# The memory tile of a transformer block: loaded in 32-token strips and turned by VectorE's block transposes, where TensorE turned it

## The reference, cut to what matters

```python
mem_n = rms_norm(mem, norm_mem_src[l])        # mem: 256 x 2048
kv = (mem_n @ w_kv).reshape(b, m, 2, MEM_HEADS, MEM_HEAD_DIM)   # w_kv: 2048 x 1024
k, v = kv[:, :, 0], kv[:, :, 1]
```

## Time and profile before

| | |
|---|---|
| median of the runs | 1356.27 us |
| the profiled execution's own time | 1355.84 us |
| its span, from the first instruction to the last | 1354.1 us |
| TensorE busy | 998.5 us (74%) |
| VectorE busy | 579.0 us (43%) |
| ScalarE busy | 300.4 us (22%) |
| GpSimd busy | 52.4 us (4%) |
| the queue of the hardware DMAs, share of 16 engines | 88.7% |
| read from HBM | 481.14 MB |
| mean granted TensorE clock | 0.873 |

### The profile page before, as it was taken

One profiled execution on the slowest core, in us unless ns is written; L12 is line 12 of the kernel. 1 busy time (PEld: TensorE's weight loads), 2 busy tenths in 40 slices (PEclk: granted clock), 3 DMA queues, 4 the chain that ended last, 5 costly groups with the idle time before them and its releaser, 6 DMA issues.

```text
span 1354.1 us, 20680 instructions
## 1 busy us (share of the span) xinstructions
PE 998.5 (74%) x8540; PEld 600.2 (44%) x8540; DVE 579.0 (43%) x1114; ACT 300.4 (22%) x521; POOL 52.4 (4%) x108
## 2 busy tenths in 40 slices
PE   8999999999999985666655566655566654566656
PEld 7888898888888532222212222222222221222222
DVE  5555566886657543223332233332223332223324
ACT  5554457674455100000000000000000000000002
POOL 1300001231000000000000000000000000000001
PEclk9999999999999998778787787787777877777878
DMA  7778763448869999999999999999999999999997
GB/s 247 263 238 255 217 167 123 144 136 273 286 252 338 358 417 428 433 430 432 433 430 434 432 432 434 433 429 433 429 434 432 433 433 433 430 432 430 433 426 303
DMA packets 78020, 486.40 MB, mean 359 GB/s; under 512 B 9943, under 2 KB 25437, under 8 KB 64798
## 3 DMA queue, kind: packets, MB, share of 16 engines
q1 hardware_dynamic: 77484, 483.46, 88.7%
q10 hardware_dynamic: 306, 2.11, 0.4%
q0 software_dynamic: 192, 0.31, 0.2%
HBM read 481.14 MB, written 4.72 MB: 359 GB/s over the span
## 4 chain that ended last, share of the span: by engine, by line
PE 51%; DMA 46%; SPq 1%; DVE 1%; issue 1%; ACT 0%; DVEq 0%; ACTq 0%
DMA gu<-in_w_up 42%; PE ps L1052 10%; PE ps L605 8%; PE ps L607 8%; PE ps L606 8%; PE ps L1107 5%; DMA down<-in_w_down 4%; PE ps L1031 2%; PE ps L1064 1%; PE ps L585 1%; PE ps L850 1%; PE ps L851 1%; PE ps L852 1%; PE ps L778 1%; SPq L470 0%
## 5 line engine op out<-in xcount | busy, mean ns | idle before, releaser
L1052 PE MATMUL ps<-gu,xe 128*32 128x256 f32 x3968 | 286.3, 452 | 306.0 <-DMA gu<-in_w_up 305.5
L2138 DVE TENSOR_TENSOR x_sum<-ps,x_sum 128x512 f32<-128x512 f32 x240 | 149.1, 684 | 507.6 <-PE ps L1064 507.6
L1052 PEld LDWEIGHTS ps<-gu,xe 128*32 128x32 f32 x3968 | 140.5, 129 | 469.3 <-DMA gu<-in_w_up 328.7
L1616 DVE TENSOR_TENSOR w_lo<-w_raw,w_hi 128x1024 fp32r<-128x1024 f32 (+1 forms) x137 | 164.6, 1208 | 118.1 <-ACT w_hi L1225 114.8
L605 PE MATMUL ps<-w_hi,a_hi 128*128 128x512 f32 (+1 forms) x468 | 183.4, 392 | 0.0
L606 PE MATMUL ps<-w_lo,a_hi 128*128 128x512 f32 (+1 forms) x468 | 179.7, 384 | 0.0
L607 PE MATMUL ps<-w_hi,a_lo 128*128 128x512 f32 (+1 forms) x460 | 176.8, 384 | 0.0
L1225 ACT ACTIVATE w_hi<-w_raw 128x1024 fp32r<-128x1024 f32 (+1 forms) x137 | 141.8, 1039 | 127.1 <-PE ps L607 88.6
L1535 ACT ACTIVATE sg<-ps 128x128 f32<-128x128 f32 x31 | 8.6, 278 | 654.3 <-PE ps L1052 654.3
L1107 PE MATMUL ps<-down,act_t 128*32 128x512 f32 x976 | 112.8, 603 | 5.3 <-DMA down<-in_w_down 5.3
L606 PEld LDWEIGHTS ps<-w_lo,a_hi 128*128 128x128 f32 x468 | 88.0, 188 | 16.4
(11 more groups left out here) (341 smaller groups left out, 854.9 us busy)
## 6 DMA issues: line engine op xcount, KB each, us to landing
down<-in_w_down SPq DMA_DIRECT2D x29, 4096.0 KB, 22.7
gu<-in_w_gate SPq DMA_DIRECT2D x28, 4096.0 KB, 31.7
gu<-in_w_up SPq DMA_DIRECT2D x28, 4096.0 KB, 41.0
w_raw<-in_w_in SPq DMA_DIRECT2D x56, 512.0 KB, 4.9
w_raw<-in_w_out SPq DMA_DIRECT2D x32, 512.0 KB, 4.7
gu<-in_w_up SPq DMA_DIRECT2D x18, 512.0 KB, 6.6
w_raw<-in_w_mem_kv SPq DMA_DIRECT2D x16, 512.0 KB, 3.5
down<-in_w_down SPq DMA_DIRECT2D x13, 512.0 KB, 15.5
```

What stands on the lines that cost most here:

```text
L1052: mm = pe.matmul(ps[5][j * SLOTS:(j + 1) * SLOTS, 0:2 * P].rearrange("s (m f) -> s m f", m=2), xe[:, k, :], gu[side][:, :, k, j * P:(j + 1 ...
L1616: ve.tensor_tensor(w_lo[:, u % RING, :, 0:n], w_raw[:, u % RING, :, 0:n], w_hi[:, u % RING, :, 0:n], ALU.subtract).then_inc(S("w_split"), 1)
L2138: ins = ve.tensor_tensor(x_sum[:, t, cols], ps[g][:, :], (x_res if first else x_sum)[:, t, cols], ALU.add)
```

## The change

Memory is loaded in eight DMAs of 32 tokens each, issued by SP behind the weight loads of units 22 to 29. A token's 2048 features are cut into four quarters q of 512, and quarter q of token s goes to partition 32q + s. A block transpose of VectorE, in place, on 128 x 512 turns each 32 x 32 block, after which partition 32q + r holds feature 512q + 32k + r of every token, in block k. So block column k is a contraction tile of 128 features (four runs of 32, from the four quarters), and the rows of w_mem_kv and the gain norm_mem_src are loaded in that order. PE's 32 transposes, their PSUM banks and the waits on them go. ACT squares eight strips of 512 elements (four after SB_K, four after SB_K+1), which leaves a sum for each quarter on each partition; POOL spreads these over a 128 x 256 tile, and two matmuls with a column of ones add them up for each token. DVE's transposes come four after SB_V and four after SB_V+1. The norm's factor moves ahead of attention on POOL's queue.

The core of the diff. Left out are the hunks that only count semaphores up by one (`sums_made`, `squares_summed`) for the new sum.

```diff
@@ -87,6 +87,7 @@
 EARLY_AT = [START[W_OUT + 2] + 4 + 2 * n for n in range(12)] + [START[MEM_Q] + 5 + n for n in range(4)]
+MEM_AT = [START[SB_Q] + 6 + _j for _j in range(SEQ // QUAD)]
 LATENT = [(c, i) for c in range(Q_PE, MEM_K) for i in range(chunk_tiles(c) // UK)]
@@ -111,7 +112,7 @@
         _b = len(SPLIT_BANK)
-        SPLIT_BANK.append(6 + _b % 2 if _name == "mem" else 4 + _b % 4)
+        SPLIT_BANK.append(None if _name == "mem" else 4 + _b % 4)
@@ -205,8 +206,11 @@
         c_kv = place("c_kv", [P, TT, KV_RANK + ROPE])
-        mem_junk = place("mem_junk", [P, D], offset=km_at)
-        mem_sb = place("mem_sb", [P, TT, D], offset=o_at)
+        mem_junk = place("mem_junk", [P, UN], offset=km_at)
+        mem_spread = place("mem_spread", [P, TT * NJ, QUAD], offset=km_at + 2048)
+        quad_eye = place("quad_eye", [P, QUAD], offset=km_at + 3072)
+        mem_quads = place("mem_quads", [P, TT * NJ, UN], offset=o_at)
+        mem_turned = mem_quads[:, :, :].rearrange("p j (k s) -> p k j s", k=KD)
         cq_hi = place("cq_hi", [P, 4, SEQ], F32R, offset=k_at)
@@ -289,7 +293,8 @@
             if MEM_K <= c <= MEM_V:
-                return [cols(w_mem_kv, (c - MEM_K) * UN)]
+                return [w_mem_kv[0, :, (c - MEM_K) * UN:(c - MEM_K + 1) * UN].rearrange(
+                    "(q k r) n -> k q r n", q=NJ, r=QUAD)[i * UK:(i + 1) * UK]]
             if c < Q_PE:
@@ -370,8 +375,11 @@
                                        (norm_sb_out, 62, 8), (norm_ffn, 70, 16)):
-                    sp.dma_start(g_nat[r0:r0 + rows, :], gain[0].rearrange("(k p) -> k p", p=P)
-                                 ).then_inc(S("gains_loaded"), 16)
+                    if gain is norm_mem_src:
+                        src = gain[0].rearrange("(q k r) -> k q r", q=NJ, r=QUAD)
+                    else:
+                        src = gain[0].rearrange("(k p) -> k p", p=P)
+                    sp.dma_start(g_nat[r0:r0 + rows, :], src).then_inc(S("gains_loaded"), 16)
                 for t in range(TT):
@@ -449,7 +457,10 @@
                 (src,) = unit_src(c, i)
-                if len(src.shape) == 4:
+                if MEM_K <= c <= MEM_V:
+                    for k in range(UK):
+                        sp.dma_start(dst[:, k, :], src[k]).then_inc(S(f"w_loaded{u % RING}"), 16)
+                elif len(src.shape) == 4:
                     for k in range(UK):
@@ -457,6 +468,10 @@
                     x_part(u)
+                if u in MEM_AT:
+                    j = MEM_AT.index(u)
+                    sp.dma_start(mem_quads[:, j, :], mem[0, j * QUAD:(j + 1) * QUAD, :].rearrange(
+                        "s (q f) -> q s f", q=NJ)).then_inc(S("mem_loaded"), 16)
                 if u in MOVE_AT:
@@ -709,15 +724,17 @@
             turn(KV_LAT)
-            pe.wait_ge(S("mem_loaded"), 16)
+            pe.wait_ge(S("mem_spread"), 1)
+            for t in range(TT):
+                mm = pe.matmul(ps[7][:, t:t + 1], mem_spread[:, NJ * t:NJ * (t + 1), :].rearrange(
+                    "p j s -> p (j s)"), ones[:, 0:1], start=True, stop=True)
+            mm.then_inc(S("squares_summed"), 1)
             for n, (c, i) in enumerate(LATENT):
...
                     project_units(c, [i], 0, hi, lo)
-                if n < KD // 2:
-                    split_turn("mem", mem_sb, 2 * n, 2 * n + 2)
                 if (c, i) == (K_NOPE + 1, 0):
@@ -1325,6 +1342,15 @@
             sc.wait_ge(S("rstd"), 1)
+            def mem_squares(t):
+                for j in range(NJ):
+                    sc.wait_ge(S("mem_loaded"), 16 * TT * NJ)
+                    square(mem_quads[:, NJ * t + j, :], chunk_ss[:, t, j:j + 1], mem_junk[:, :])
+                    sq[0] += 1
+                    sc.wait_ge(S("squared"), sq[0])
             for c in range(Q_LAT, Q_PE):
@@ -1336,9 +1362,6 @@
                     squares_of(c_kv[:, :, 0:KV_RANK], SS_KV, junk[:, 0:KV_RANK])
-                    sc.dma_start(mem_sb[:, :, :], mem[0].rearrange("(t p) d -> p t d", p=P)).then_inc(
-                        S("mem_loaded"), 16)
                 elif c < SB_V:
@@ -1350,20 +1373,25 @@
                     chunk_copy(c, lambda t: v_sb[:, t, n0:n0 + UN], SS_X)
+                if SB_K <= c < SB_V:
+                    mem_squares(c - SB_K)
                 if c == SB_K:
...
                     split_head("kv", 52, hi=ckv_hi)
-            def mem_squares(t):
-                square(mem_sb[:, t], sums[:, SS_MEM + t:SS_MEM + t + 1], mem_junk[:, :])
-                sq[0] += 1
-                sc.wait_ge(S("squared"), sq[0])
+            def mem_heads(k):
+                if k == 0:
+                    sc.wait_ge(S("w_used"), START[Q_PE])
+                    sc.wait_ge(S("split_turned"), (SPLIT0["mem"] + KD) // 2)
+                sc.activation(a_hi[:, k, :].rearrange("p (j s) -> p j s", s=QUAD), mem_turned[:, k], ACT.Copy,
+                              scale=g_t[:, 16 + k:17 + k]).then_inc(S("split_hi"), 1)
...
                 if n < KD // 2:
-                    split_head("mem", 16, START[Q_PE], k_from=2 * n, k_to=2 * n + 2)
+                    mem_heads(2 * n)
+                    mem_heads(2 * n + 1)
                 if POS[(c, i)] + 1 < DONE[c]:
@@ -1726,8 +1750,17 @@
                              ALU.max).then_inc(S("angles"), 1)
+            def turn_mem(t):
+                ve.wait_ge(S("squared"), 3 * TT + NJ * (t + 1))
+                for j in range(NJ * t, NJ * (t + 1)):
+                    ve.transpose(mem_quads[:, j, :], mem_quads[:, j, :]).then_inc(S("split_turned"), 1)
             for c in range(Q_LAT, Q_PE):
                 split_w(DONE[c] + RING)
+                if c >= SB_V:
+                    turn_mem(c - SB_V)
                 if c == SB_K + 1:
@@ -1746,10 +1779,23 @@
             copy_turned(KV_LAT)
+            def mem_rest(k):
+                ve.wait_ge(S("split_hi"), SPLIT0["mem"] + k + 1)
+                ve.scalar_tensor_tensor(
+                    out=a_lo[:, k, :].rearrange("p (j s) -> p j s", s=QUAD), in0=mem_turned[:, k],
+                    scalar=g_t[:, 16 + k:17 + k],
+                    in1=a_hi[:, k, :].rearrange("p (j s) -> p j s", s=QUAD), op0=ALU.mult,
+                    op1=ALU.subtract).then_inc(S("split_lo"), 1)
+            ve.wait_ge(S("squares_summed"), 1)
+            ve.tensor_copy(sums[:, SS_MEM:SS_MEM + TT], ps[7][:, 0:TT]).then_inc(S("sums_made"), 1)
             for n, (c, i) in enumerate(LATENT):
...
                 if n < KD // 2:
-                    split_rest("mem", 16, k_from=2 * n, k_to=2 * n + 2)
+                    mem_rest(2 * n)
+                    mem_rest(2 * n + 1)
                 if (c, i) in ROPE_AT:
@@ -2321,6 +2367,18 @@
             scale_latent(c_kv, KV_RANK, SS_KV, 3)
+            for q in range(1, NJ):
+                link(gp.tensor_tensor(quad_eye[:, :], ident[:, 0:QUAD] if q == 1 else quad_eye[:, :],
+                                      ident[:, q * QUAD:(q + 1) * QUAD], ALU.add))
+            gp.wait_ge(S("squared"), 3 * TT + TT * NJ)
+            gp.tensor_tensor(
+                mem_spread[:, :, :],
+                quad_eye[:, :].rearrange("p (a s) -> p a s", a=1).to_broadcast([P, TT * NJ, QUAD]),
+                chunk_ss[:, :, :].rearrange("p t j -> p (t j)").rearrange(
+                    "p (j a) -> p j a", a=1).to_broadcast([P, TT * NJ, QUAD]),
+                ALU.mult).then_inc(S("mem_spread"), 1)
+            norms([SS_MEM], D, "sums_made", 1)
             def diagonals(v):
@@ -2343,8 +2401,6 @@
                                      diagonals(sb_mask[:, :]), ALU.mult).then_inc(S("sb_masked"), 1)
-                if i == 1:
-                    norms([SS_MEM], D, "squared", 4 * TT)
                 if 3 <= i < HEADS:
```

More of the change, by code:

```diff
@@ L391, in early_piece @@
                     sp.wait_ge(S("out_lo"), KD)
-                    sp.wait_ge(S("sums_made"), 1)
+                    sp.wait_ge(S("sums_made"), 2)
                 if n < 8:
@@ L828, in _ @@
                 if q == 1:
-                    pe.wait_ge(S("sums_made"), 1)
+                    pe.wait_ge(S("sums_made"), 2)
                 split_turn("memx", x_res, 4 * (q - 1), 4 * q)
@@ L1381, in _ @@
                     chunk_copy(c, lambda s: v_mla[:, s, t * UN:(t + 1) * UN])
-                    if t == 0:
-                        mem_squares(t)
             def head_square(h):
@@ L1427, in _ @@
                     rounded(START[MEM_K] + 2 * i + RING)
-                if i == 0:
-                    mem_squares(1)
                 if i == 3:
@@ L1824, in _ @@
             out_rest(7)
-            ve.wait_ge(S("squares_summed"), 1)
+            ve.wait_ge(S("squares_summed"), 2)
             ve.tensor_copy(sums[:, SS_A:SS_A + 2 * TT], ps[6][:, 0:2 * TT]).then_inc(S("sums_made"), 1)
@@ L2361, in _ @@
                 S("router_loaded"), 16)
-            norms([SS_A, SS_B], HEADS * HD, "sums_made", 1)
-            norms([SS_X1], D, "sums_made", 2)
+            norms([SS_A, SS_B], HEADS * HD, "sums_made", 2)
```

(3 more changed lines are left out.)

## The result

The changed kernel takes **1373.48 us** (median; 1372.99 to 1375.75), the kernel before 1356.49 us in the runs beside it: ratio 1.0129, 95% interval 1.0112 to 1.0147. The forecast was 1372.6 us. The profiled execution took 1373.13 us, its span is 1371.4.

The account below looks back on a forecast made before the run. TensorE bounds the kernel until about 470 us, then the expert weight loads. Stalls of 8.0 + 6.7 + 2.1 = 16.8 us on 1355.84 gave 1372.6 us, the saved transposes bringing nothing; range 1352 to 1386.

Parts of the forecast that it names:

- Four engines: Memory and w_mem_kv loads, outermost dimension 4, share the same four of 16 DMA engines; chance 0.72, 1372.6 us.
- First place: Units 22 to 31: memory pieces on four engines make unit 32 late, a TensorE stall of 8.0 us.
- the bound of 10.9: Upper bound of the stall at unit 32, in us, with packets of 96.7 ns.
- Second place: The 16 w_mem_kv units in attention: four engines make unit 89 late by 6.7 us (0 to 13.5).
- my lower bound of 82.5: Lowest assumed time in ns for a 2 KB packet on its engine, from a full queue; 90 was taken.
- Third place: Unit 90, loaded after MEM_K's quarters are moved behind unit 89: a TensorE wait of 2.1 us (1.2 to 2.3).
- The transposes: Eight groups of TensorE transposes removed, 0.44 us each, 3.5 us; the saving brings nothing while TensorE waits behind them.
- the wait for the bank: At K_NOPE+1 TensorE arrives about 0.2 us before ScalarE has emptied its bank.
- The two matmuls: Added on TensorE, with a 128x1 result: 0.4 us.
- The covers: New ScalarE, VectorE and GpSimd work stays hidden under TensorE; VectorE's row after SB_V+1 fits by 0.8 us.
- the third case of the rivals: 16 engines, but VectorE's cover after SB_V+1 fails: three hold-ups, 3.1 us, take the gain, 1356; chance 0.05.
- The rival with sixteen engines: All loads keep 16 engines, leaving only TensorE's gain of 2.9 us, 1352.9; chance 0.23.

Follow-up runs that it names:

- kv_over_2: mem_over_16 with the rows of w_mem_kv read as 2 groups of 64 (outermost 2) instead of 4 of 32; 1441.5 us, ratio 1.0622.
- mem_over_16: The changed kernel with each memory load taking one quarter of four strips (outermost 32, not 4), w_mem_kv unchanged; 1361.0 us, ratio 1.0035.
- kv_over_8: mem_over_16 with the rows of w_mem_kv read as 8 groups of 16 (outermost 8) instead of 4 of 32; 1355.0 us, ratio 0.9995.
- kv_over_16: The changed kernel with each w_mem_kv unit in four 128 KB loads (outermost 32), not two with outermost 4; 1367.5 us, ratio 1.0090.
- both_over_16: The changed kernel with both memory and w_mem_kv loaded with 32 outermost; 1356.2 us, ratio 0.9996.
- pieces_128_rows: both_over_16 with each memory load putting 128 tokens on 128 partitions, not four strips on 32; 1354.1 us, ratio 0.9984.

## Why the prediction was right

**Four engines** was the step that carried it, and kv_over_2, mem_over_16 and kv_over_8 show it. The inference from g_row's missing landing was thin evidence for it (it speaks for fewer than sixteen engines, and not for four) and true: with the pieces over sixteen engines the landings are there again.

**First place**, forecast 8.0, measured 12.5. The mechanism was right, step by step. Unit 32 was ready at 102.55 (its split's end), forecast 99.1. Of the 3.4 us, 1.6 are a later issue of unit 22 (51.19; 0.9 of it is the start of the kernel, no loss). From there to the landing of the spill, 93.9, it took 42.7 us where I had 41.2 (432 packets and a landing), and unit 32 from its issue to its rounding 4.5 where I had 4.1. That is 10.8 us of DMA, inside the bound of 10.9. The missing term is the clock, 1.7 us behind the stall: no row of before had TensorE wait, so I had no price for what comes after a wait, and I hadn't asked for one. Neither part is fixed: kv_over_16, the same program up to there, lost no time to the clock at unit 32 and 11.8 us to the DMAs, above that bound.

**Second place**, forecast 6.7 at unit 89, measured 4.2 at units 75 and 76. The packet was mis-sized: 77 ns where the four engines have nothing else to do, below my lower bound of 82.5, which came from a queue that other loads shared. At 77 ns the unit takes 4.9 us and attention's 5.0 is kept. And I had compared with attention's pace only; ahead of it TensorE uses a unit in under 3 us.

**Third place**, forecast 2.1: unit 90 was in time in the kernel after, and its late rounding cost 1.0 us at unit 92. In mem_over_16, where TensorE was less delayed by the second place, unit 90 came 1.3 us late and unit 92 another 1.5. With sixteen engines for w_mem_kv neither appears. So the term exists and depends on the others.

**The transposes**, forecast 3.5 us for eight groups, and nothing in the sum. They count, since TensorE doesn't wait at unit 89. In both_over_16 units 64 to 72 take 2.6 us less than before; the wait for the bank is in that. Before, at the first group:

```profile
182.49 0.60 PE L585 MATMUL ps<-ident,mem_sb 128*128 128x128 f32 x4
182.85 0.48 PE L605 MATMUL ps<-w_hi,cq_hi 128*128 128x512 f32 x1
```

That is 0.36 us to the next matmul, which takes 0.09 longer than its neighbours. So the chain's 0.44 was right for this group, and for the two after it, but the next three brought 0.34 each. The two matmuls came to 0.45 (0.4), the bank's wait to 0.2 as forecast: 0.45 - 2.6 = -2.15 in the kernels with sixteen engines for w_mem_kv. The kernel after has -1.95, since unit 74 starts 0.2 us late there: the second place begins with it.

**The covers.** VectorE's block transposes took 670 ns, where half of the earlier trace rows is 618, and the residues show no hold-up, so the third case of the rivals did not happen. The transposes in the kernel after (min/median/max ns):

```profile
L1758 DVE STREAM_TRANSPOSE mem_quads<-mem_quads x8: 668/670/705, 173.6 to 197.1; 128x512 f32<-128x512 f32 x8
```

The residues, likewise:

```profile
L1786 DVE SCALAR_TENSOR_TENSOR a_lo<-mem_quads,g_t,a_hi x16: 474/477/480, 198.7 to 218.7; 128x256 fp32r<-128x256 f32 x16
```

**The rival with sixteen engines**, 1352.9. Built as both_over_16 it gives 1356.2, and as pieces_128_rows, with no partitions crowded, 1354.1. The rival had a gain of 2.9 us on TensorE, where 2.15 came, and no term for a load that writes 32 partitions. It also said that the packets of memory stay at 2 KB. In the kernel before they were 8 KB, as the queue that carried them shows at 45 to 60 us:

```profile
q10 hardware_dynamic: 234, 1.92, 31.5%
```

234 packets for 1.92 MB, 0.315 x 16 x 15 / 234 = 323 ns for each, four times a small one's, so it cost the sum nothing.

**Left open.** mem_over_16 and both_over_16 are the same program up to unit 74, and their profiled runs lost 5.8 and 2.4 us in the first place, with packets of 153 and 123 ns. The one also had a stretch of low clock at unit 28, but TensorE waited another 1.5 us for unit 32 behind it, so it hardly adds to the loss; why the packets differed was not tried. Nor was the condition for the low clock.

## What to carry to other kernels

When a load is rearranged, read its outermost dimension on both sides before its bytes: 4 there means four of sixteen DMA engines, for this load and for all others queued behind it on those. Cut such a load so that 16 or a multiple stands outermost (32 and 128 here), and then ask how many partitions one load covers, for 32 are slower than 128 even with all engines. And when a load is moved, move it against its first reader's place in the reader's queue, not against the time of its use.

## What I had not expected of the hardware

- The issue itself is held. While the few engines of a load are behind, SP's issue instruction takes as long as the load needs, 2.46 us with four engines, 5.0 with two, 0.6 with eight, and everything behind it on SP waits too.
- A 2 KB packet took 77 ns on four engines of their own (kernel after, w_mem_kv), 88 to 95 ns in a mixed queue over all sixteen (pieces_128_rows, before), and 123 to 153 ns when loads into 32 partitions ran beside the weights (both_over_16, mem_over_16).
- After three waits of 2.1 to 3.2 us TensorE came back at 1.2 GHz in the kernel after, and lost 1.7 us over the unit behind each. Not each such wait does it: in mem_over_16 one of 2.2 us at the start of attention was followed by a clock of 1.00, and in kv_over_16 one of 3.3 us ahead of unit 32.
- A transfer on fewer than sixteen engines shows no landing in the view of DMA issues, and takes the landing from others that share its semaphore: w_raw<-in_w_in, 4.9 us before and still on all engines, has none in the kernel after, and has it again (5.6 us) in both_over_16.
